# A tenth weight tile in the expert stage: gate matrices of experts 3, 7 and 11 in the work area, and one selection buffer

## The reference, cut to what matters

```python
N_EXPERTS, EXPERT_FF, D_MODEL, SEQ = 32, 512, 1024, 512
...
g_sel = jnp.argmax(g_logits, axis=-1)                 # one of 4 groups
top_val, top_idx = lax.top_k(e_logits[tok, g_sel], 2) # two of its 8 experts
gate = p_group[:, None] * jax.nn.softmax(top_val, axis=-1)
...
def expert_block(args):
    rows, e = args
    xb = x_pad[rows]
    return (jax.nn.silu(xb @ w_gate[e]) * (xb @ w_up[e])) @ w_down[e]
```

## Time and profile before

| what | value |
|---|---|
| median of 3 runs | 1664.09 us (1663.37 to 1664.76) |
| the profiled execution: time | 1666.44 us |
| the profiled execution: span | 1664.3 us, granted TensorE clock 0.982 |
| busy: PE, PEld, DVE, ACT, POOL | 94%, 49%, 38%, 26%, 23% of the span |
| moved | 468.77 MB, mean 282 GB/s |
| expert stage of layer 0 | from about 332 us (router done) to 820 us |
| expert stage of layer 1 | from about 1154 us to 1643 us |

### The profile page before, as it was taken

How to read it: one execution, slowest core, us unless ns; L and a number is a source line. 1 busy time by engine, 2 the same in 40 slices (tenths; PEclk the granted TensorE clock), 3 DMA queues, 4 the chain that set the end, 5 groups by cost and what they waited for, 6 DMA issues and landing times.

```text
span 1664.3 us, 20438 instructions
## 1 busy us (share of the span) xinstructions
PE 1556.2 (94%) x8292; PEld 821.3 (49%) x8292; DVE 629.5 (38%) x1226; ACT 430.9 (26%) x778; POOL 374.5 (23%) x440
## 2 busy tenths in 40 slices
PE   8999999979999999998799999998999999999975
PEld 4655666546444444443356546655554444444422
DVE  1686635471221222211417856364512211222115
ACT  3554740211111111111235647303111111111112
POOL 5472860000000000000364539400000000000003
PEclk9999999989999999999999999999899999999998
DMA  9200303659999999999930012065699999999996
GB/s 395 118 1 13 140 1 86 272 208 401 412 427 427 428 426 426 427 427 427 362 151 1 1 41 113 1 196 234 250 371 421 426 427 426 427 428 426 429 428 245
DMA packets 54082, 468.77 MB, mean 282 GB/s; under 512 B 18985, under 2 KB 19113, under 8 KB 27458
## 3 DMA queue, kind: packets, MB, share of 16 engines
q1 hardware_dynamic: 46738, 451.12, 65.6%
q0 software_dynamic: 7104, 16.24, 2.7%
q10 hardware_dynamic: 144, 0.07, 0.0%
HBM read 446.44 MB, written 26.74 MB: 284 GB/s over the span
## 4 chain that ended last, share of the span: by engine, by line
PE 73%; DMA 18%; DVE 5%; ACT 2%; issue 1%; POOL 0%; SPq 0%; POOLq 0%; DVEq 0%
PE bank L884 20%; DMA ring<-wu 18%; PE bank L551 11%; PE bank L914 9%; PE bank L687 7%; PE bank L876 6%; PE bank L860 2%; PE bank L626 2%; PE bank L545 2%; PE bank L613 2%; PE bank L641 2%; PE bank L522 1%; PE bank L901 1%; PE bank L741 1%; PE bank L539 1%
## 5 line engine op out<-in xcount | busy, mean ns | idle before, releaser
L884 PE MATMUL bank<-ring,hbuf 128*64 128x512 f32 x704 | 312.8, 598 | 21.8 <-DMA ring<-wu 21.8
L885 PE MATMUL bank<-ring,hbuf 128*64 128x512 f32 x704 | 313.2, 599 | 0.0
L2046 POOL DMA_INDIRECT expert_rows<-raw_qd,store_rows x60 | 58.8, 980 | 1066.1 <-ACT raw_qd L1276 894.9
L1799 DVE COPY raw_qd<-bank 128x256 f32<-128x256 f32 x64 | 27.2, 425 | 699.4 <-PE bank L901 696.7
L551 PE MATMUL bank<-hbuf,ring 128*128 128x512 f32 x480 | 210.0, 594 | 0.0
L884 PEld LDWEIGHTS bank<-ring,hbuf 128*64 128x64 f32 x704 | 95.8, 138 | 220.9 <-issue 220.8
L914 PE MATMUL bank<-ring,raw_qd 128*64 128x512 f32 x352 | 160.5, 598 | 5.2 <-DVE raw_qd L1799 4.1
L884 PE MATMUL bank<-raw_qd,hbuf 128*64 128x512 f32 x320 | 145.9, 610 | 16.2 <-DMA hbuf<-wu 13.9
L916 PE MATMUL bank<-ring,raw_qd 128*64 128x512 f32 x352 | 160.5, 598 | 0.0
L876 PE MATMUL bank<-raw_qd,x 128*128 128x192 f32 x896 | 159.5, 332 | 0.0
L1269 ACT ACTIVATE raw_qd<-bank 64x512 f32<-64x512 f32 x64 | 37.8, 590 | 445.7 <-PE bank L885 445.7
(11 more groups left out here) (374 smaller groups left out, 2251.0 us busy)
## 6 DMA issues: line engine op xcount, KB each, us to landing
ring<-wg SPq DMA_DIRECT2D x44, 2048.0 KB, 22.9
ring<-wu SPq DMA_DIRECT2D x44, 2048.0 KB, 27.7
ring<-wd SPq DMA_DIRECT2D x44, 2048.0 KB, 26.6
ninth_slot<-wd SPq DMA_DIRECT2D x20, 2048.0 KB, 27.6
hbuf<-wu SPq DMA_DIRECT2D x20, 2048.0 KB, 27.6
raw_qd<-wg SPq DMA_DIRECT2D x20, 2048.0 KB, 22.9
ring<-w_in SPq DMA_DIRECT2D x8, 2048.0 KB, 14.2
ring<-w_out SPq DMA_DIRECT2D x4, 2048.0 KB, 8.5
```

The source lines that it names most:

```text
L884: mm(pb[2 + par][0:CAP, :], tokens[:, k, :], gates[:, k, :], start=(k == 0), stop=(k == KT - 1))
L885: last = mm(pb[2 + par][CAP:P, :], tokens[:, k, :], ups[:, k, :], start=(k == 0), stop=(k == KT - 1))
L2046: G.indirect_dma_start(out=half_rows, out_offset=bass.IndirectOffsetOnAxis(ap=store_i[:, e:e + 1], axis=0), in_=y_sb[e % 2], in_offset=Non ...
```

## The change

A tenth tile is added: 128 x 3584 floats of `raw` (columns 3584 to 7168) and 128 x 512 of `hbuf` (columns 5632 to 6144) together hold one gate matrix. Until expert 11, gates rotate over four slots (0, 3, 6 and the new 9), from expert 12 over three again. Gate 3 is issued after the router products and before the wait for `dest`; in the loop, step e issues gate e+1 in place of gate e for e = 3 to 13, no gate at e = 14, and gate e from e = 15 on. A gate in slot 9 is loaded by two transfers, one of 14 KB rows and one of 2 KB rows. To free the place, one `pick` buffer remains, `second` moves to `hbuf`, the temporaries move together, and the selections are written anew: for group 0 as before, for the others four instructions that compare the first choice, four that compare the second and add it in place, and four that multiply by 1/rms. Each waits for the last pick part of the group before it, and they run in steps e = 0 (group 1) and e = 2, 6, 10, ... (group e/4 + 2). Last, the semaphore of the final rows is merged with another.

```diff
+FOUR_GATES = 12
...
-        pick = [raw[:, 1024 * i:1024 * i + NB * GC].rearrange("p (b s) -> p b s", b=NB) for i in range(2)]
-        slot_ids = raw[:, 6656:6656 + GC]
+        pick = raw[:, 0:NB * GC].rearrange("p (b s) -> p b s", b=NB)
+        slot_ids = raw[:, 768:768 + GC]
...
-        second = raw[:, 2048:2048 + NB * GC].rearrange("p (b s) -> p b s", b=NB)
+        second = hbuf[:, 6144:6144 + NB * GC].rearrange("p (b s) -> p b s", b=NB)
...
+        TENTH = (raw[:, 3584:7168], hbuf[:, 5632:6144])
+        W_gate = {3 * i: [tile(slot_tile[3 * i], FF * k, FF) for k in range(KT)] for i in range(3)}
+        W_gate[9] = [tile(TENTH[0], FF * k, FF) for k in range(KT - 1)] + [TENTH[1]]
...
+        def gate_slot(e):
+
+            return (0, 3, 6, 9)[e % 4] if e < FOUR_GATES else 3 * (e % 3)
...
+            def gate_weights(e):
+                to = gate_slot(e)
+                if to == 9:
+                    sp.dma_start(TENTH[0], wg[base + e, :, 0:FF * (KT - 1)]).then_inc(slot[9], 16)
+                    sp.dma_start(TENTH[1], wg[base + e, :, FF * (KT - 1):FF * KT]).then_inc(slot[9], 16)
+                else:
+                    sp.dma_start(slot_tile[to], wg[base + e]).then_inc(slot[to], 16)
...
             sp.dma_start(ring[:, 5, :], wd[base + 1]).then_inc(slot[5], 16)
+            sp.wait_ge(s["rms2"], on("rms2") + 1)
+            sp.wait_ge(s["rlT"], on("rlT") + NB)
+            gate_weights(3)
             sp.wait_ge(s["dest"], on("dest") + 2)
...
                 sp.wait_ge(s["gu"], e - 2)
-                sp.dma_start(slot_tile[at], wg[base + e]).then_inc(slot[at], 16)
+                if e + 1 < FOUR_GATES + 3:
+                    gate_weights(e + 1)
+                elif e >= FOUR_GATES + 3:
+                    gate_weights(e)
                 sp.dma_start(slot_tile[at + 1], wu[base + e]).then_inc(slot[at + 1], 16)
...
-            def selection(group):
-
-                if group >= 2:
-                    dve.wait_ge(s["xp"], GRP * (group - 1))
...
+            def selection(group):
+                link(TS(rel_at, small[:, 0:2 * NB], -float(GC * group), None, ALU.add))
+                dve.wait_ge(s["xp"], GRP * group)
+                ids = slot_ids[:, 0:GC]
+                for b in range(NB):
+                    ins = TS(pick[:, b, :], ids, rel_at[:, b:b + 1], None, ALU.is_equal)
+                link(ins)
+                for b in range(NB):
+                    ins = STT(out=pick[:, b, :], in0=ids, scalar=rel_at[:, NB + b:NB + b + 1], in1=pick[:, b, :],
+                              op0=ALU.is_equal, op1=ALU.add)
+                link(ins)
+                for b in range(NB):
+                    TS(pick[:, b, :], pick[:, b, :], rstd[:, b:b + 1], None, ALU.mult).then_inc(s["oh"], 1)
...
-            selection(1)
...
                     hidden_rows(e + 1)
-                if e % GRP == 0 and e // GRP + 2 < NGRP:
+                if e == 0:
+                    selection(1)
+                if e % GRP == 2 and e // GRP + 2 < NGRP:
                     selection(e // GRP + 2)
```

More of the change, by code:

```diff
@@ L217, in trunk @@
         xT = [hbuf[:, 4096 + 2048 * i:4096 + 2048 * i + KT * GC].rearrange("p (k c) -> p k c", k=KT) for i in range(2)]
[L218 to L226, removed]
+        e_e, e_s = (raw[CAP * i:CAP * i + CAP, 1024:1536] for i in range(2))
+        hid = [raw[CAP * i:CAP * i + CAP, 1536:2048] for i in range(2)]
+        hidT = [raw[:, 2048 + 256 * i:2304 + 256 * i].rearrange("p (k c) -> p k c", k=FT) for i in range(2)]
+        y_sb = [tile(raw, 2560 + 512 * i) for i in range(2)]
+        gathered = [raw[:, at:at + 1024] for at in (0, 4608, 5632, 7168, 8192)] + [
+                    qd[:, 0:1024], qd[:, 1024:2048], hbuf[:, 4096:5120]]
+        weighted, weighted_t = (raw[:, 4608 + 512 * i:5120 + 512 * i].rearrange("p (b s) -> p b s", b=NB) for i in range(2))
+        selT = [tile(raw, at) for at in (3584, 4096)]
         rel_late = small[:, 8:16]
@@ L239, in trunk @@
         s_rstd = sem("its_inverse_root")
-        s_fd = sem("final_rows")
         s_out = sem("out_stored")
@@ L293, in trunk @@
             dn="PE: down", ye="ACT: expert rows evacuated", cb="PE: weighted selections turned, rows combined",
-            cv="DVE: weighted selections built, those evacuated", moe="DVE: MoE residual")
+            cv="DVE: weighted selections built, those evacuated", moe="DVE: MoE residual, at last the final rows of a block")
         BY_LAYER = ("xp", "xp_e", "gu", "ee", "ec", "hid", "ht", "ht_e", "dn", "ye", "oh", "oc",
@@ L301, in trunk @@
             kv_e=4, r_ln=5, r_rs=5, ho_s=2, ex=16, ho_r=3, pt_e=16, bt_e=4, ke=8, y5_e=1, gx=4, h2_a=4,
-            rlT_e=4, rms2=1, gx2=1, sx=1, ev_d=9, dve=174, lb=3, h_k=4, q_silu=4, h_c=4, head=4, r_y=5, hs_m=4,
+            rlT_e=4, rms2=1, gx2=1, sx=1, ev_d=9, dve=160, lb=3, h_k=4, q_silu=4, h_c=4, head=4, r_y=5, hs_m=4,
             r_done=5, state=4, mx=16, pn=16, o_a=2, pn_e=16, o_b=16, ct=1, res=16, bt_v=4, xr=8, z=4,
@@ L309, in trunk @@
         slot_third = [sem(f"slot{i}") for i in range(6, 9)]
-        slots = [slot_even + [sem(f"slot{i}_{j}") for i in range(3, 6)] + slot_third for j in range(L)]
+        tenth = [sem("tenth_slot")]
+        slots = [slot_even + [sem(f"slot{i}_{j}") for i in range(3, 6)] + slot_third + tenth for j in range(L)]
         y_out = [sem(f"y_rows{i}_stored") for i in range(2)]
@@ L362, in trunk, with gate_loaded @@
         slot_tile = [ring[:, i, :] for i in range(6)] + list(THIRD)
-        W_gate = [slot_tile[3 * i].rearrange("p (k c) -> p k c", k=KT) for i in range(3)]
+        TENTH = (raw[:, 3584:7168], hbuf[:, 5632:6144])
+        W_gate = {3 * i: [tile(slot_tile[3 * i], FF * k, FF) for k in range(KT)] for i in range(3)}
+        W_gate[9] = [tile(TENTH[0], FF * k, FF) for k in range(KT - 1)] + [TENTH[1]]
         W_up = [slot_tile[3 * i + 1].rearrange("p (k c) -> p k c", k=KT) for i in range(3)]
         W_down = [slot_tile[3 * i + 2].rearrange("p (k c) -> p k c", k=FT) for i in range(3)]
+        def gate_slot(e):
+            return (0, 3, 6, 9)[e % 4] if e < FOUR_GATES else 3 * (e % 3)
+        def gate_loaded(e, layer):
+            mine = [i for i in range(NE) if gate_slot(i) == gate_slot(e)]
+            before = 0 if gate_slot(e) == 3 else len(mine) * layer
+            return (32 if gate_slot(e) == 9 else 16) * (before + mine.index(e) + 1)
         def loaded(slot_, e, layer):
@@ L859, in pick_half @@
                             pe.wait_ge(s["oh"], NB * half + b + 1)
-                        last = mm(pb[n % 2][:, WIN * i:WIN * i + WIN], x[:, b, P * k:P * k + P], pick[0][:, b, slots],
+                        last = mm(pb[n % 2][:, WIN * i:WIN * i + WIN], x[:, b, P * k:P * k + P], pick[:, b, slots],
                                   start=(b == 0), stop=(b == NB - 1))
@@ L875, in pick_part @@
                     for b in range(NB):
-                        last = mm(pb[n % 2][:, GC * i:GC * i + GC], x[:, b, P * k:P * k + P], pick[group % 2][:, b, :],
+                        last = mm(pb[n % 2][:, GC * i:GC * i + GC], x[:, b, P * k:P * k + P], pick[:, b, :],
                                   start=(b == 0), stop=(b == NB - 1))
@@ L883, in gate_up_of @@
                         pe.wait_ge(s["xp_e"], 2)
-                    mm(pb[2 + par][0:CAP, :], tokens[:, k, :], gates[:, k, :], start=(k == 0), stop=(k == KT - 1))
+                    mm(pb[2 + par][0:CAP, :], tokens[:, k, :], gates[k], start=(k == 0), stop=(k == KT - 1))
                     last = mm(pb[2 + par][CAP:P, :], tokens[:, k, :], ups[:, k, :],
@@ L891, in gate_up @@
                 i = 3 * (e % 3)
-                pe.wait_ge(slot[i], loaded(i, e, layer))
+                pe.wait_ge(slot[gate_slot(e)], gate_loaded(e, layer))
                 pe.wait_ge(s["xp_e"], e + 1 if e < 2 else GRP * (e // GRP) + GRP)
@@ L896, in gate_up @@
                 pe.wait_ge(slot[i + 1], loaded(i + 1, e, layer))
-                gate_up_of(e % 2, xT[e // GRP % 2][:, :, at:at + CAP], W_gate[e % 3], W_up[e % 3], halves=(e == 0))
+                gate_up_of(e % 2, xT[e // GRP % 2][:, :, at:at + CAP], W_gate[gate_slot(e)], W_up[e % 3], halves=(e == 0))
             def hidden_of(par, first=0):
@@ L968, in tensor_program @@
                 with pe.Fori(0, n_over) as i:
-                    gates_loaded = pe.snap((i + (NE + 1) // 3 + 1) * 16)
+                    gates_loaded = pe.snap(i * 16 + gate_loaded(NE - 1, 0) + 16)
                     loaded_later = pe.snap((i + (NE + 1) // 3 + 2) * 16)
@@ L981, in tensor_program @@
                     pe.wait_ge(slot[4], loaded_later)
-                    gate_up_of(1, xT[1][:, :, 0:CAP], W_gate[1], W_up[1])
+                    gate_up_of(1, xT[1][:, :, 0:CAP], W_gate[3], W_up[1])
                     pe.wait_ge(s["hid"], pe.snap(i + NE + 1))
@@ L1711, in vector_program, with first_selection @@
             link(TT(rel_all, rel_all, at_row, ALU.add))
-            def selection(group):
-                if group >= 2:
```

(18 more changed lines are left out.)

## The result

The changed kernel takes 1653.22 us (median of 4 runs, 1651.1 to 1655.59) against 1663.73 us for the kernel before in the same comparison. The ratio is 0.9938, with a 95% interval of 0.9924 to 0.9952: 10.3 us less, between 8.0 and 12.6. The forecast was 1654.7 us.

A forecast was written before the change was run, and what follows sets the result against it. PE sets the pace early in each expert stage, then the continuous stream of loads sets its end. Span 1664.3 - 9.8 + 0.4 = 1654.9 us; from the median of 1664.09, 1654.7 us, range 1651.4 to 1660.8.

The forecast's parts named there:

- The sum: Whole kernel: -9.8 us for the tiles and +0.4 us for the two-part loads, giving 1654.7 us from the median.
- A tile per layer: Expert stages: the tenth tile gains one tile's transfer, 4.9 us, per layer, -9.8 us for two layers.
- A tile moved into that gap leaves the stream one tile shorter.: Before the continuous loads of layer 0, some 17 us lie idle during DVE's router bookkeeping; loading a tile there shortens the stream.
- only if the queue doesn't run dry there: Step 14, where a gate is left out: condition for the later tiles to stand 4.9 us earlier in the queue.
- 7.4 us of remaining work at step 14: Load queue where a gate is left out: 12.3 us of work less 4.9 us leaves 7.4 us, growing each step.
- the first rival: The lead is lost at expert 14 because the queue runs dry or gate 3 is late: 1664.5 us, chance 0.06.
- The selections: DVE's selections in the expert stage: 4 to 5 us each, hidden under covers of 8.6 and 10.85 us, cost 0.
- only groups 1 and 2 could reach the end: A selection 1 us over its cover delays PE 1 us; only these groups, ahead of 437 us, could affect the end.
- The two-part loads: Gates 7 and 11 of each layer: four extra small transfers at 0.1 us each, +0.4 us, range 0 to 6.4.
- The rivals with a fixed part in a full queue: Extra transfers in the queue cost 8 us (1662.3 us, chance 0.03) or 16 us (1670.3 us, slower 0.05).
- The signs to look for: Profile after: gate load near 332 us, up-matrix waits some 12 and 14 us, first at expert 24 or 25, layer end near 815.
- The dip of the clock after the last load: PE's clock at 0.55 over 3 us costs 1.35 us per layer; it may vanish or double, +-2.7 us.

The follow-up runs named there:

- e8: The kernel before, unedited, run once more for a second trace: 1664.66 us, one run.
- e1: The changed kernel again, unedited, as reference of its group of runs: 1655.37 us against 1665.15 for the kernel before, ratio 0.9946.
- e3: Changed kernel with gate 3 issued behind gate 2, after the wait for dest, out of the idle stretch: 1656.46 us, ratio 0.9957 to the kernel before.
- e4: Changed kernel with gate 3 still early but no gate issued at step 3, gate e from step 4: 1665.25 us, ratio 1.0003 to the kernel before.
- e2: Changed kernel with its new selections but without the tenth tile, gate 3 loaded in step 3: 1665.51 us, ratio 1.0004 to the kernel before.
- e7: Changed kernel with the first compare of the selections repeated ten times for groups 3 to 6: 1655.62 us, ratio 0.9944 to the kernel before.
- e6: Changed kernel with every gate for experts 3 to 31 loaded in two transfers: 1657.64 us, ratio 0.9957 to the kernel before.
- e5: Changed kernel with the lead given up at step 8 in place of step 14: 1658.46 us, ratio 0.9956 to the kernel before.

## Why the prediction was right

**The sum.** Forecast -9.8 + 0.4 = -9.4 us; measured -10.3 (-12.6 to -8.0) and -9.0 us (-11.3 to -6.5). The sum had the right size. The terms by themselves are the next points.

**A tile per layer.** Right in size: the waits for loads fell by 5.2 and 6.4 us, and between the second traces (e8 and e1) by 4.1 and 4.9. By the start of expert 31 in layer 0 the gain is 801.50 - 795.10 = 6.4 us, of which 0.3 us was there before the stage (gate 2 issued at 358.39 against 358.73). That is more than the 4.9 us of a tile; the early windows of the two pairs of traces (399 against 393, 396 against 384 GB/s) would make 0.7 to 1.4 us, and that is within what the same code scatters. Some 0.5 us of the first pair has no source that was found. The second traces give stage lengths, as measured under e3, of 443.0 and 441.1 us for the kernel before (e8) and 436.8 in both layers for the changed one (e1). So from trace to trace the gain of a layer reads 4.3 to 6.2 us, around the tile's 4.9. The difference of the two profiled spans, 13.5 us, is thus in part chance.

**"A tile moved into that gap leaves the stream one tile shorter."** This sentence was the weak step. For the change as it was made it holds: the early window kept its gaps, and from step 14 on the queue held one tile less. But the gap alone is neither enough for the gain nor needed for it, as e4 and e3 show. With the tile in the idle stretch but the lead given up at step 3, nothing is gained; with the tile out of it but the lead kept to step 14, 7.2 of 9.0 us remain. What the change brings is a tenth tile that may be under way: PE's steps free one place at a time, and each place is refilled at a moment that PE sets, so a queue that runs dry before 437 us passes on none of what was saved before. The gain comes when the lead is given up with work in the queue. The prediction did say this as a condition ("only if the queue doesn't run dry there"), and its 7.4 us of remaining work at step 14 held: 427 GB/s through step 14, and a clear loss at steps 8 (1.9 us of transfer) and 3 (4.8 us), where the queue is shorter. So what the first rival described, a queue that runs dry where the gate is left out, does happen, at step 3 and in part at step 8, but not at step 14. What the prediction did not see is that the same gain, to 1 or 2 us, comes without the idle stretch: a tile queued behind gate 2 fills the dry moments before 437 us instead.

**The selections.** Right: no cost that e2 can show. Their length was overestimated, 4 to 5 us against 3.5: the fused form takes 0.35 us (1.40 us for four), not 0.45, and the shift of the token places, counted in the 13 instructions, now runs before DVE waits for the picks. The cover was even more generous than stated: for groups 3 to 6 the selection may outlast it by over 2 us at no cost (e7). The prediction had said so: only groups 1 and 2 could reach the end.

**The two-part loads.** Right in size: 0.03 to 0.09 us each against 0.1, measured on 52 more of them. The four of the change itself are too few to be seen. The rivals with a fixed part in a full queue (+8 and +16 us) fall with e6.

**The signs to look for.** The waits of 11.9 and 12.2 us against some 12 and 14, the first at expert 24, and the early gate load at 332 us came as said. The layer's combination on PE starts at 812.1 us in the first trace and at 814.8 in e1 (it was at 820.3, forecast near 815). The dip of the clock after the last load, a part of the range, was not there in layer 0 of the first profiled execution, where the last wait is 1.65 and not 3.35 us. It goes with that wait in all ten traces of layer 0: the three whose last wait is 1.6 us (this one, e2 and e3) show no dip, and the seven with a last wait of 3.3 to 3.4 us do (in e1 the mean granted clock over the same 4 us is 0.71). In the changed kernel:

```profile
796.00:800.00 4.00, 4.00 (x22) 1.69 (x20) 0.00 (x0) 2.24 (x3) 0.00 (x0) 1.00 0.97 410
```

The chain also moved at the end of that layer, which had not been foreseen: it goes through the stored and gathered rows instead of the last down product. In the chain of the changed kernel:

```profile
794.88 7.97 DMA expert_rows<-raw_qd,store_rows
...
807.48 5.66 DMA raw_qd<-expert_rows,dest_i
```

In e3, also without a dip, the chain goes the same way. In e1, with a dip and so a later PE, it is again that of the up matrix of expert 31. The combination on PE starts 2.7 us later in e1 than in the first trace, but PE begins the next layer only 1.0 us later (825.73 against 824.70 us): what PE gained in the first trace it waited for the rows. So the two paths lie close together, and a further tile of lead would probably be worth less than the first unless the rows come earlier too. That was not tried.

## What to carry to other kernels

- Where a stage starts bound by compute and ends bound by loads, its end is set by when the stream of loads became continuous. Here one more buffer was worth one transfer, because it was kept until the queue held more work than that transfer; given back in a nearly dry queue it was worth nothing (e4), in between a part (e5).
- To look for an idle stretch of the transfer engines isn't enough. Ask at which moments places come free, and whether the queue still runs dry between them.
- Work put on an engine's path in the part of a stage where that engine has waits ahead can come out of these waits: here 9.5 us in each layer, of some 12, cost nothing that the median shows.

## What the runs showed of the hardware

- A 256 KB transfer in 2 KB rows, queued behind others, costs 0.03 to 0.09 us beyond its bytes, though a lone tile takes some 4 us more than its bytes to land.
- The rate at which the same code fills its transfer engines while the queue is nearly dry varies between executions, 385 to 399 GB/s over 51 us, while the full queue reads 427 over the 190 us from 437 on, in every trace but those of e5 (423, lead given up at step 8) and e6 (425, every gate in two parts). This scatter, up to 1.7 us per layer, may be a part of the several us by which runs of one kernel differ; that was not tested.
- PE's granted clock fell for a few us (to 0.55 over 3 us in the kernel before) after a wait of 3.3 to 3.4 us ahead of expert 31, in seven traces of layer 0, and stayed at 1.00 after one of 1.6 us, in three.
